# Stick-breaking heads of the mixer: value products in pairs, and scores of heads 2 to 5 split over both halves of the TensorE rows, through copies with exchanged rows made by DMA

## The reference

```python
def stick_breaking_attention(q, k, v):
    """A[t,s] = sigmoid(z_ts) * prod_{s<j<t} (1 - sigmoid(z_tj)), s < t, in log space."""
    ...
        valid = kpos[None, :] < (start + jnp.arange(Q_BLOCK))[:, None]
        z = jnp.einsum('bhqd,bhkd->bhqk', a, k, preferred_element_type=jnp.float32)
        log_fail = jnp.where(valid, jax.nn.log_sigmoid(-z), 0.0)
        after = lax.cumsum(log_fail, axis=3, reverse=True) - log_fail
        wts = jnp.where(valid, jnp.exp(jax.nn.log_sigmoid(z) + after), 0.0)
        return jnp.einsum('bhqk,bhkd->bhqd', wts, v, preferred_element_type=jnp.float32)

def token_mixer_2(h, w_in, w_out, lam_params, subln_gain, layer):
    proj = h @ w_in
    ...
    mixed = jnp.concatenate([from_heads(o_a), from_heads(o_b), from_heads(o_c)], axis=-1)
    return mixed @ w_out
```

## Time and profile before

| | |
|---|---|
| Time, median of 3 (lowest, highest) | 3336.99 us (3336.99, 3346.36) |
| Time of the profiled execution | 3350.7 us |
| Its span, first to last instruction | 3348.8 us, mean granted clock of TensorE 0.980 |
| PE busy | 3169.2 us (95%) |
| DVE busy | 1861.8 us (56%) |
| ACT busy | 1261.1 us (38%) |
| PE share of the chain that ended last | 74% |
| Stage `stick` of the two layers | about 1877 to 1942 us and 2885 to 2949 us |

### The profile page before, as it was taken

The page is one execution under the profiler, slowest core; times in us unless marked ns, Lnnn a source line. Parts: engine busy times, 40 slices in busy tenths (PEclk is TensorE's granted clock), DMA queues, the critical chain, the costliest instruction groups (busy, mean ns, idle before and its releaser), DMA issues.

```text
span 3348.8 us, 60877 instructions
## 1 busy us (share of the span) xinstructions
PE 3169.2 (95%) x26440; PEld 2493.3 (74%) x26440; DVE 1861.8 (56%) x2741; ACT 1261.1 (38%) x2098; POOL 179.6 (5%) x168
## 2 busy tenths in 40 slices
PE   7999789999998888999999999999999999999999
PEld 6866677875443234999876679988999876679987
DVE  4366656557121114886355358854886355358853
ACT  3227433322000002453345544433443345544432
POOL 0003222221000000000000000000000000000000
PEclk8999799999999999999999999999999999999999
DMA  7140000114999996333321113323233321123322
GB/s 268 51 151 25 3 4 4 57 34 164 396 407 422 421 421 266 101 101 114 113 82 51 51 63 114 114 96 106 89 113 114 114 82 51 51 63 114 105 92 88
DMA packets 179764, 441.64 MB, mean 132 GB/s; under 512 B 7602, under 2 KB 107692, under 8 KB 154924
## 3 DMA queue, kind: packets, MB, share of 16 engines
q1 hardware_dynamic: 179500, 437.74, 35.4%
HBM read 435.62 MB, written 2.10 MB: 131 GB/s over the span
## 4 chain that ended last, share of the span: by engine, by line
PE 74%; DMA 8%; DVE 6%; ACT 3%; issue 2%; POOL 0%; SPq 0%; DVEq 0%; POOLq 0%; ACTq 0%
PE banks L3624 7%; PE banks L3622 7%; PE banks L3625 7%; PE banks L4023 7%; PE banks L2734 5%; PE banks L3744 4%; PE banks L3742 4%; PE banks L3743 4%; DMA ring<-in_exp_w_down 3%; DMA ring<-in_exp_w_gate 3%; DMA ring<-in_exp_w_up 1%; PE banks L350 1%; PE banks L394 1%; PE banks L1818 1%; PE banks L1673 1%
## 5 line engine op out<-in xcount | busy, mean ns | idle before, releaser
L2734 PE MATMUL banks<-ring,arena 128*64 128x512 f32 x1120 | 262.5, 605 | 36.8 <-DMA ring<-in_exp_w_gate 13.8
L3744 PE MATMUL banks<-tail_r,hid_r 128*128 128x512 f32 x704 | 278.3, 395 | 0.0
L3742 PE MATMUL banks<-tail_r,two_r 128*128 128x512 f32 x640 | 254.3, 397 | 0.0
L3743 PE MATMUL banks<-ring_r,two_r 128*128 128x512 f32 x640 | 248.0, 388 | 0.0
L2734 PEld LDWEIGHTS banks<-ring,arena 128*64 128x64 f32 x1120 | 86.1, 139 | 199.8 <-issue 185.4
L3622 PE MATMUL banks<-ring_r,tail_r 128*128 128x256 f32 x624 | 175.7, 282 | 9.1 <-DVE arena L3707 9.1
L305 DVE TENSOR_TENSOR hid_r<-arena,two_r 128x1024 fp32r<-128x1024 f32 x40 | 49.1, 1227 | 235.7 <-ACT two_r L302 221.4
L3624 PE MATMUL banks<-h_r,tail_r 128*128 128x256 f32 x624 | 175.7, 282 | 0.0
L3624 PE MATMUL banks<-ring_r,tail_r 128*128 128x256 f32 x624 | 175.5, 281 | 0.0
L3622 PE MATMUL banks<-mix_r,tail_r 128*128 128x256 f32 x624 | 174.3, 279 | 0.0
L3625 PE MATMUL banks<-ring_r 128*128 128x256 f32 x608 | 171.4, 282 | 0.0
(11 more groups left out here) (611 smaller groups left out, 8627.2 us busy)
## 6 DMA issues: line engine op xcount, KB each, us to landing
ring<-in_exp_w_gate SPq DMA_DIRECT2D x62, 1024.0 KB, 23.0
ring<-in_w_ffn_gate SPq DMA_DIRECT2D x44, 1024.0 KB, 5.4
ring<-in_w_ffn_up SPq DMA_DIRECT2D x44, 1024.0 KB, 5.4
ring<-in_exp_w_down SPq DMA_DIRECT2D x40, 1024.0 KB, 23.2
ring<-in_w_ffn_down SPq DMA_DIRECT2D x20, 2048.0 KB, 7.9
ring<-in_exp_w_up SPq DMA_DIRECT2D x38, 1024.0 KB, 19.0
ring<-in_w_in SPq DMA_DIRECT2D x13, 2048.0 KB, 10.1
arena<-in_exp_w_up SPq DMA_DIRECT2D x26, 1024.0 KB, 23.5
```

The lines of the kernel that those rows point to most:

```text
L2734: ins = TE.matmul(banks[64 * e:64 * e + 64, b0 + hf, :], lhs(kk, e), w[:, k, hf * 512:(hf + 1) * 512], start=(kk == 0), stop=(kk == KD - 1))
L3742: TE.matmul(bank, h_hi, w_hi[:, c, ns], start=(f == 0), stop=False)
L3743: TE.matmul(bank, h_hi, w_lo[:, c, ns], start=False, stop=False)
L3744: ins = TE.matmul(bank, h_lo, w_hi[:, c, ns], start=False, stop=(f == NF - 1))
```

## The change

1. The value products of heads 2p and 2p + 1 are issued in turn, tile by tile, into the two halves of the rows of one bank (`values(p, tiles_)`), and one copy takes both out (`out_copy(l, p)`). There are 3 pairs instead of 6 heads.
2. For heads 2 to 5 the scores of key tiles 1 and 3 (384 and 128 columns) read `swapped`, a copy of the queries and keys in which rows 0 to 63 and 64 to 127 have changed places, so that they run in the other half of the rows than tiles 0 and 2 (512 and 256 columns). The copy is made by four DMAs of 64 rows x 1024 words (256 KB each), issued by SP behind the loads of `w_out`. `z(2)` waits for it.
3. The last of the 28 groups leaves the filling and stands between after_sums(0) and z(2).
4. The order in `st_pe` is new, `clamped` is cut in two (512 columns, then 768), z(i + 2) waits for the first cut, and the logarithm and exponential of the norm move on ScalarE from turn 2 to turn 3.
5. `wt` has four homes instead of two, two of them in places that were used by the softmax heads; the ring slot that holds `swapped` and one home is given free after the last pair of value products.

```diff
-                    LAST = len(gs) - NT
+                    LAST, END = len(gs) - NT, len(gs) - 1
...
+                    bank_at[len(gs) - 1], bank_free[len(gs) - 1] = 6, last_in[6]
...
-                    wt = region(hT_at + 1536, 2, 1280)
+                    wt_homes = [region(sb_at, 1280), region(body + 3 * T, 1280), region(hT_at + 1536, 1280), region(hT_at + 2816, 1280)]
+                    wt = lambda h: wt_homes[h % 4]
...
                     wos = [stream(wo_src[:, 4 * s_:4 * s_ + 4, :], (4, D)) for s_ in range(2)]
-                    slot_user[first % RING] = (nm, "all_turned", N - 1)
+                    slot_user[first % RING] = (nb, "pv", 2)
+                    swapped = region(swap_at, 4, T)
+                    small(nm + "swapped", [(swapped[o:o + HD, 2 * e:2 * e + 2, :], qk[HD - o:P - o, 11 + 3 * e:13 + 3 * e, :])
+                                           for e in range(2) for o in (0, HD)],
+                          when=[(nm, "all_turned", N - 1)] + [(nm, "read", group_of["qk", i]) for i in (11, 12, 14, 15)])
...
                         if i >= 2:
-                            l.wait_ge(*past(nb, "clamped", i - 2))
+                            l.wait_ge(*past(nb, "clamped0", i - 2))
+                            if i == 2:
+                                l.wait_ge(*smalls[nm + "swapped"])
...
+                            if s_ == 1 and i >= 2:
+                                l.wait_ge(*past(nb, "clamped", i - 2))
+                            if i >= 2 and s_ in (1, 3):
+                                rows, keys, queries = slice(HD - half(i), P - half(i)), swapped[:, 1 + i // 2, :], swapped[:, i // 2 - 1, :]
+                            else:
+                                rows, keys, queries = rows_of(i), qk[:, 13 + i // 2, :], qk[:, 10 + i // 2, :]
...
+                            for j in tiles_:
                                 oj = where[j][2]
+                                for h in (2 * p, 2 * p + 1):
+                                    po = half(h)
+                                    ins = TE.matmul(banks[po:po + HD, 6 + p % 2, j * P:T], vt[:, j, 640 + h * HD:640 + (h + 1) * HD],
+                                                    wt(h)[:, oj:oj + T - j * P], start=(j == 0), stop=(j == NT - 1))
...
                         z(l, 1)
-                        for i in range(6):
+                        after_sums(0)
+                        part_of_group(l, len(gs) - 1, 0, len(gs[-1]["mms"]))
+                        z(l, 2)
+                        after_sums(1)
...
+                        z(l, 3)
+                        for i in (2, 4):
                             after_sums(i)
+                            values(i // 2 - 1, (0,))
+                            if i == 2:
+                                z(l, 4)
+                            after_sums(i + 1)
+                            values(i // 2 - 1, (1, 2, 3))
+                            if i == 2:
+                                z(l, 5)
...
-                            if i == 2:
+                            if i == 3:
                                 l.wait_ge(*past(nb, "sub_var"))
                                 l.did(S.activation(rs2, sq2, ACT.Ln).then_inc(l.sem, 1))
...
+                                for key, c0, c1, ended_ in (("zc0", 0, T, "clamped0"), ("zc", T, 1280, "clamped")):
+                                    l.wait_ge(*past(nb, key, h))
+                                    l.did(V.tensor_scalar(wt(h)[:, c0:c1], flat(h)[:, c0:c1], 0.0, None, ALU.min).then_inc(l.sem, 1), nb, ended_, h)
```

More of the change, by code:

```diff
@@ L4002, in beside @@
                             split_unit(l, u, k0, k1)
-                    def w_pe(l):
[L4005 to L4027, removed]
@@ new lines, in part_of_group @@
+                    def part_of_group(l, i, j0, j1):
+                        g = gs[i]
+                        if j0 == 0:
+                            if i == 0:
+                                for t in (2, 3):
+                                    l.wait_ge(*past(early, "lo", t))
+                            l.wait_ge(ring_full[g["loads"][0] % RING], g["loads"][1])
+                            l.wait_ge(*past(nm, "lo", g["unit"]))
+                            if i >= OPEN and bank_free[i] is not None:
+                                l.wait_ge(*past(nm, "read", bank_free[i]))
+                            elif i >= OPEN and bank_of(i) == 5:
+                                k_, g_ = [kg for kg in turn_no if turn_bank(*kg) == 5][-1]
+                                l.wait_ge(*past(nm, "T", k_, g_))
+                        for m in g["mms"][j0:j1]:
+                            bank = banks[:, bank_of(i), :]
+                            if i < 2:
+                                ins = TE.matmul(m[1](bank)[:, T // 2:T], m[2], m[3][:, T // 2:T], start=m[4], stop=m[5])
+                            else:
+                                ins = TE.matmul(m[1](bank), m[2], m[3], start=m[4], stop=m[5])
+                        if j1 == len(g["mms"]):
+                            l.did(ins.then_inc(l.sem, 1), nm, "made", i)
+                            l.name_last(nm, "used", g["unit"])
+                            l.name_last("freed", g["loads"][0])
@@ L4305, in after_sums @@
                                                     start=False, stop=(m == later[s_][-1][0]), skip_group_check=True)
+                                if s_ == 0:
+                                    l.did(ins.then_inc(l.sem, 1), nb, "zc0", i)
                             l.did(ins.then_inc(l.sem, 1), nb, "zc", i)
[L4308 to L4315, removed]
-                                oj = where[j][2]
-                                ins = TE.matmul(banks[po:po + HD, 6 + h % 2, j * P:T], vt[:, j, 640 + h * HD:640 + (h + 1) * HD],
-                                                wt[:, h % 2, oj:oj + T - j * P], start=(j == 0), stop=(j == NT - 1))
-                            l.did(ins.then_inc(l.sem, 1), nb, "pv", h)
@@ new lines, in st_pe @@
+                        z(l, 1)
+                        after_sums(0)
+                        part_of_group(l, len(gs) - 1, 0, len(gs[-1]["mms"]))
+                        z(l, 2)
+                        after_sums(1)
+                        l.wait_ge(*past(nb, "squares"))
+                        l.wait_ge(*past(nm, "read", len(gs) - 1))
+                        for k in range(2):
+                            ins = TE.matmul(banks[:, 6 + k, :], ones2, sq2[:, k, :], start=True, stop=True)
+                        l.did(ins.then_inc(l.sem, 1), nb, "sub_sums")
@@ L4412, in split_out @@
                     def split_out(l):
[L4413 removed]
+                        l.wait_ge(*past(nb, "o", 2))
                         for u in range(2, KD // 2):
```

85 lines of the change are left out of this document (42 added, 43 removed).

## The result

The changed kernel takes 3354.3 us in the median of seven runs (3351.99 to 3358.69) against 3344.0 for seven runs of the kernel before (3336.99 to 3348.51). The medians are 10.3 us apart. The ratio over these runs is recorded as 1.0038, 95% interval 1.0027 to 1.005: slower by about 0.4%, and clear of no change. The profiled execution took 3358.69 us with a span of 3356.9.

The account below looks back on a forecast made before the run. TensorE's own work was taken to bound the stage `stick`. Terms summed to +0.1 us in layer 0 and +1.5 in layer 1, plus 4.0 for one second clock fall: +5.6 on the 3336.99 median, 3343 us, range 3326 to 3356.

Parts of the forecast that it names:

- slow copies: Rival, chance 0.22: SBUF-to-SBUF copies take 8.1 us instead of 4.0, each stall before z(2) is 16.4, time 3351 us.
- the forecast's own case: Chance 0.60: none, one or both layers have a second clock fall, giving 3339, 3343 or 3347 us.
- What bounds the kernel: In the stage `stick`, TensorE's own work is the price, so shortening it pays if nothing else comes late.
- The hole ahead of z(2) and its half rate go: TensorE's 2.71 us wait for head 0's clamp and the low clock behind it vanish: -7.5 us layer 0, -6.1 layer 1.
- The group as filling, z(1) 4.40 us earlier: The last group's 24 matmuls, 4.40 us, move from before z(1) to behind after_sums(0), so z(1) starts that much earlier.
- The stall 12.3: TensorE idles before z(2): 0.1 us for SP, 8.2 for `w_out`, 4.0 for copies; 12.3 per layer (10.8 to 16.4).
- 2.15 lost at half rate behind it: After the stall before z(2), 4.3 us at half clock, costing 2.15 us per layer (at most 4.8).
- A second fall in one of the two layers: The 2.2 us hole before z(5) drops the clock again in one layer, costing 4.0 us.
- Pairs of values, -6.0: Value products of two heads in turn take 2.6 us instead of 4.6; three pairs save 6.0 us per layer.
- Scores on both halves, -3.0: Overlapping row halves cut each score z from 2.35 to 1.6 us; four heads save 3.0 us per layer.
- the copies do not wait: Rival, chance 0.12: copies before z(2) land beside `w_out`, 3329 us, or are there when z(2) asks, 3314 us.
- scores do not overlap: Rival, chance 0.06: z stays at 2.35 us, +3.0 per layer, the hole before z(5) shrinks to 1.45; 3343 us.

Follow-up runs that it names:

- copies ahead: The changed kernel with the four row-exchanged copies issued ahead of the second half of `w_out` instead of behind it; 3321.81 us.
- the group back: Against the kernel called both: the last group back among the filling ahead of z(1), where it was before the change; 3314.83 us.
- the late copies: The changed kernel with the four copies still issued after the last group ends, but ahead of the second half of `w_out`; 3345.77 us, one run.
- own rows and splits later: The changed kernel with scores of heads 2 to 5 on their own rows, no copies, and the `w_out` and `mixed` splits one turn later; 3314.88 us.
- both: The changed kernel with the copies issued ahead of the second half of `w_out` and the `w_out` and `mixed` splits one turn later; 3317.23 us.
- own rows with unpaired values: Against own rows and splits later: value products of a pair issued one head after the other instead of in turn; 3323.25 us.
- six matmuls ahead of z(1): Two kernels, both and own rows and splits later, each with 6 of the last group's 24 matmuls ahead of z(1); 3314.51 and 3315.96 us.

## Why the prediction went wrong

It said no change within 0.3%, at 3343 us; the kernel became slower by 0.4%, for which the chance given was 0.28, 0.19 of it by slow copies and 0.08 by the forecast's own case. The waits were the ones forecast, one by one. What failed is the price of the clock behind them: the half rate behind the stall was put at 2.15 us and measured 3.4 and 3.5, and the second fall, put at 4.0 once, came in both layers at 3.4 each. The stall itself was 0.75 to 1.1 too short, a small hole ahead of z(1) was left out, and the base was low.

- *What bounds the kernel:* right. Where the stall and the low clock behind it went, as with copies ahead, the stage became shorter by as much, and the growth of the stage covers the difference of the kernels.
- *The hole ahead of z(2) and its half rate go* (-7.5, -6.1): right, but not only for the reason given. With the group back there is no hole ahead of z(2) either, only 0.7 us inside it. The norm's two matmuls, of which the prediction said that they only change places, no longer hold up the clamp behind z(2), and the cut clamp starts early; how the hole divides between the two is not shown.
- *The group as filling, z(1) 4.40 us earlier:* 3.56. The group takes 4.25 us in its new place, and TensorE waited 0.67 for the read of bank 5. The step left that wait out, so that moving the group costs 0.7 where it was put at nothing.
- *The stall 12.3:* 13.36 and 13.05. The order of the queue, the landing of `w_out` and the copies behind it were as said. Less the 0.1 and the 8.2 of the sum, 5.1 and 4.75 are left for the copies where 4.0 was taken, though from 1887 to 1890 us the queue moved 291 down to 242 GB/s, on both sides of the 264 assumed. Alone they held z(2) back for 6.8 us, issue and completion included. The Trainium skill (SBUF — State Buffer, "Door 1: The DMA port swizzle") gives 196 GB/s for 1 MiB over partitions 0 to 63, from which the prediction estimated a stall of 13.6. That is nearer, but in part by luck, since the rate in the trace is higher.
- *2.15 lost at half rate behind it:* 3.4 and 3.5. This is the first term that failed. I had scaled by the hole of 5.23, after which 4.3 us ran at half rate; after 13.4 it was 6.8 and 7.0, after the 6.8 of the late copies 7.3 and 6.4. The two cases inside this very stage, 4.8 and 3.4 us lost, were the nearer rows. What TensorE loses depends on when in the hole the clock falls and how long it stays low. At 346 it was low from 344.2 to 351.06, 6.8 us, of which 2.5 fell into the hole; in the change it was low for 17.1 us, 1882.3 to 1899.4, of which 10.3 fell into the stall. What sets these lengths was not found out.
- *A second fall in one of the two layers:* in both. This term failed too: 3.4 twice where I had put 4.0 once. The hole ahead of z(5), 2.38 us, was forecast well (2.2). But the chance of a fall was weighed against one hole of 2.09 without one, and the runs show falls behind 2.38 and 1.51 in every layer that had such a hole.
- *Pairs of values, -6.0:* -6.6. The three pairs of the changed kernel took 2.5, 2.5 and 2.3, where six heads took 13.8. It adds up in layer 1 of the kernel with own rows and splits later, which is 94.93 - 82.76 = 12.2 us shorter than before: the hole of 2.71, 3.4 of clock and 6.6 for the pairs, less 0.7 for the hole ahead of z(1), make 12.0.
- *Scores on both halves, -3.0:* -3.4 by their own durations, but worth 1.8 where nothing else is wrong. The hole that it feeds was seen for z(5) alone.

Per layer the forecast sum was +0.1 and +1.5 without a second fall; measured +5.8 and +7.0. In layer 0 the excess of 5.7 is 1.1 (stall) + 1.25 (half rate behind it) + 3.4 (second fall) + 0.2 (second hole) + 0.7 (ahead of z(1)), less 1.0 from scores and pairs: 5.6. In layer 1: 0.75 + 1.35 + 3.4 + 0.2 + 0.7 - 1.0 = 5.4 against 5.5. Over both layers the stage grew by 7 us more than the +5.6 that had one second fall in it. The clock's two terms make 5.4 of these, 2.6 behind the stall and 2.8 for the second falls. The base adds 7.0: the median of three runs was 3336.99, that of seven 3344.0. The two together are 14, the distance from 3343 to 3354.3 is 11.3, since the medians moved by 10.3 and the stages by 12.8; both lie within the interval. The time lies inside the range given, but the range reached so far up for slow copies with a second fall, which is not what happened.

Of the rivals, the slow copies came true in small part: 5.1 us behind `w_out` by the prediction's own sum, against 4.0 taken, 8.1 as the bound and about 6 from which they would have made the kernel slower by themselves. That the copies do not wait, or that scores do not overlap, is refuted by the rows above.

## What to carry to other kernels

When the bottleneck engine waits for a transfer, price it with everything ahead of it on its queue, if the queue works in order as SP's does here. Before shortening the transfer, look whether it can be issued ahead of a load that still waits for its slot and that no one needs yet. Swapping these two issues turned +0.4% into -0.65%. And when matmuls are shortened, walk the chain of the other engines first: here ScalarE and VectorE were so close to setting the pace that the exchanged rows, the costliest part of the change to build, brought 1.8 of 3.4 us per layer, and the version without them can't be told from it (3314.88 against 3317.23).

## What the runs showed of the hardware

The clock is touched by much shorter holes than I had thought, and not each time. After 2.38 us it fell in all cases (two layers each of after, of copies ahead and of copies late), after 1.51 us in both layers, for 6.8 us in one and 3.4 in the other. After the 0.82 and 0.51 us late in the stage it never fell. The hole of 0.67 us ahead of z(1) stands in nine of these kernels, 18 layers in all. It was followed by a fall of 3.4 us in four of them: layer 0 of copies ahead, of both and of copies late, and layer 1 of own rows with unpaired values. This is the busy time by stretch of the kernel with copies ahead, behind its z(1) at 1866.38:

```profile
1868.00:1869.00 1.00, 1.00 (x8) 0.67 (x6) 0.00 (x0) 0.00 (x0) 0.00 (x0) 1.00 0.00 0
1869.00:1870.00 1.00, 1.00 (x5) 0.65 (x5) 0.00 (x0) 0.55 (x1) 0.00 (x0) 0.59 0.00 0
...
1872.00:1873.00 1.00, 1.00 (x4) 0.74 (x3) 0.45 (x1) 0.00 (x0) 0.00 (x0) 0.70 0.00 0
```

TensorE is busy throughout while the clock is low, so the fall costs 1.7 us that no idle time shows. In the three kernels without the hole (six matmuls ahead of z(1), or the group back) there was no fall in six layers. With four falls in 18 layers, none in six can be chance, so that the 0.67 causes the fall is not shown.

Four copies from SBUF to SBUF of 256 KB over 64 partitions land in 4.1 us in the median when they go first, and 9.9 when they stand behind 2 MB:

```profile
ring<-in_w_out SPq DMA_DIRECT2D x2, 2048.0 KB, 8.5
ring<-arena SPq DMA_DIRECT2D x4, 256.0 KB, 9.9
...
ring<-arena SPq DMA_DIRECT2D x4, 256.0 KB, 4.1
```

These are the DMA issues from 1780 to 2080 us, by median time to landing: the first two lines of the changed kernel, the last of the kernel with copies ahead.
